# Four recurrent mixers on one Trainium2 core: three groups of small products move in the order of the engines

## What is computed

```python
p = jnp.einsum('btd,dc->btc', h, w_in[l]).astype(F32)
pa, pb, pc, pd = _split(p, MIXER_COLS)
ya = _hgrn2_mixer(pa, lb_all[l], hgrn_norm_g[l])
yb = _gla_mixer(pb, gla_gate_w2[l], gla_gate_b[l], gla_norm_g[l])
...
yc, v_first = _rwkv7_mixer(pc, v_first, v_mix, rwkv_mu[l], rwkv_w0[l], rwkv_w2[l],
...
yd = _retnet_mixer(pd, positions, log_gamma)
mix = jnp.einsum('btc,cd->btd', jnp.concatenate([ya, yb, yc, yd], axis=-1), w_out[l])
```

```python
log_f = jax.nn.log_sigmoid(g_lr @ gate_w2 + gate_b) / GLA_GATE_NORM
...
scores = jnp.einsum('bhik,bhjk,bhijk->bhij', qi, ki, decay)
out = (jnp.einsum('bhij,bhjv->bhiv', scores, vi)
       + jnp.einsum('bhik,bhkv->bhiv', qi * jnp.exp(cum), state))
```

## Time and profile before

| what | value |
|---|---|
| median of 3 runs | 3372.28 us (3362.64 to 3374.18) |
| the profiled execution | 3374.25 us, its span 3372.5 us |
| PE busy | 3001.1 us, 89% of the span |
| PEld busy | 2630.4 us, 78% |
| DVE, ACT, POOL busy | 1614.0, 1079.4 and 96.5 us |
| granted clock of PE, mean | 0.909 |
| mixer stage of layer 0 | 213.4 to 436.7 us |
| mixer stage of layer 1 | 1122.0 to 1348.2 us |
| granted clock in each of the two | 0.77 |

### The profile page before, as it was taken

How to read it: one execution, slowest core, us unless ns; L and a number is a source line. 1 busy time by engine, 2 the same in 40 slices (tenths; PEclk the granted TensorE clock), 3 DMA queues, 4 the chain that set the end, 5 groups by cost and what they waited for, 6 DMA issues and landing times. The chain is left out here.

```text
span 3372.5 us, 42029 instructions
## 1 busy us (share of the span) xinstructions
PE 3001.1 (89%) x16604; PEld 2630.4 (78%) x16604; DVE 1614.0 (48%) x2073; ACT 1079.4 (32%) x1405; POOL 96.5 (3%) x92
## 2 busy tenths in 40 slices
PE   7999977999799998769999999959999685769997
PEld 6889876878578897769999999948878574758786
DVE  3436544242443356446676767763232336542333
ACT  3334113222222331135455545542222313232222
POOL 0012100000000211000000000000000000000000
PEclk9988788999899877869999999979999896789998
DMA  4210015142232000146666666634241210141521
GB/s 147 82 40 1 1 63 138 56 131 60 66 102 76 15 1 1 63 133 184 193 191 176 190 189 193 193 100 122 70 119 38 88 35 2 55 136 44 144 59 63
DMA packets 438967, 316.87 MB, mean 94 GB/s; under 512 B 22577, under 2 KB 395313, under 8 KB 438705
## 3 DMA queue, kind: packets, MB, share of 16 engines
q1 hardware_dynamic: 438832, 314.96, 32.7%
HBM read 312.29 MB, written 2.62 MB: 93 GB/s over the span
## 5 line engine op out<-in xcount | busy, mean ns | idle before, releaser
L1424 PE MATMUL psum<-x_split,gate_up_split 128*128 128x512 f32 x1056 | 415.9, 394 | 39.2 <-DVE gate_up_split L1500 31.2
L1425 PE MATMUL psum<-x_split,gate_up_split 128*128 128x512 f32 x1056 | 414.7, 393 | 0.0
L1426 PE MATMUL psum<-x_split,gate_up_split 128*128 128x512 f32 x1056 | 414.3, 392 | 0.0
L2405 PE MATMUL psum<-x_slots_split,gate_up_split 128*128 128x320 f32 x1424 | 377.7, 343 | 7.5 <-DVE gate_up_split L2549 5.6
L1709 PE MATMUL psum<-w_split,x_split 128*128 128x256 f32 (+1 forms) x2400 | 300.7, 288 | 32.6 <-DVE w_split L1743 25.9
L1709 PEld LDWEIGHTS psum<-w_split,x_split 128*128 128x128 f32 x2400 | 296.4, 197 | 37.9 <-ACT w_split L1723 26.7
L1709 PE MATMUL psum<-x_split,w_split 128*128 128x512 f32 x1248 | 297.4, 398 | 25.1 <-DVE w_split L1743 19.9
L2406 PE MATMUL psum<-x_slots_split,gate_up_split 128*128 128x160 f32 x1424 | 314.9, 241 | 0.0
L1709 PEld LDWEIGHTS psum<-x_split,w_split 128*128 128x128 f32 x1248 | 237.2, 192 | 85.8 <-ACT w_split L1723 22.2
L1522 DVE TENSOR_TENSOR arena<-arena,psum 128x512 f32<-128x512 f32 x66 | 45.4, 688 | 530.0 <-ACT arena L1483 530.0
L2405 PEld LDWEIGHTS psum<-x_slots_split,gate_up_split 128*128 128x128 f32 x1424 | 261.9, 189 | 13.6 <-ACT gate_up_split L2490 5.8
(11 more groups left out here) (411 smaller groups left out, 4622.0 us busy)
## 6 DMA issues: line engine op xcount, KB each, us to landing
arena<-in_moe_w_gate SPq DMA_DIRECT2D x91, 512.0 KB, 4.5
arena<-in_moe_w_up SPq DMA_DIRECT2D x91, 512.0 KB, 5.8
arena<-in_moe_w_down SPq DMA_DIRECT2D x176, 256.0 KB, 3.9
arena<-in_ffn_w_gu SPq DMA_DIRECT2D x88, 512.0 KB, 5.3
arena<-in_w_in SPq DMA_DIRECT2D x36, 1024.0 KB, 5.3
arena<-in_ffn_w_down SPq DMA_DIRECT2D x132, 256.0 KB, 3.7
arena<-in_ffn_w_gate SPq DMA_DIRECT2D x22, 512.0 KB, 4.1
arena<-in_ffn_w_up SPq DMA_DIRECT2D x22, 512.0 KB, 5.5
```

The lines of the kernel that those rows point to most:

```text
L1424: nc.tensor.matmul(out, w[0], XR[:, 0, k, :], start=k == 0, stop=False)
L1425: nc.tensor.matmul(out, w[0], XR[:, 1, k, :], start=False, stop=False)
L1426: mm = nc.tensor.matmul(out, w[1], XR[:, 0, k, :], start=False, stop=k == DT - 1)
L2405: hi = lambda start, stop: nc.tensor.matmul(out, wt[0], XE[:, k8, :, :].rearrange("p s n -> p (s n)"), start=start, stop=stop)
```

## The change

Three groups of small PE work move, with what reads them, and one moves to another place in PSUM.

- `E.pe_swap` stands first on PE, ahead of `R.pe_scores(0)`.
- `L.pe_gate` and `L.dve_bias` stand behind `E.pe_state(2)` and `E.dve_state(2)`.
- `pe_diagonal` of H stands behind level 6 and ahead of `R.pe_solve_x(6)`; that of L stands ahead of level 6. Both now also wait for `corners` 1, that is for `act_take(5)`, since the diagonal now lands in bank 3, which level 5 used; before it landed in bank 1 behind the transposed keys. `act_diagonal` stands ahead of `act_take(6)`, and the two counts of `turned` and `kt_ready` change places.

```diff
--- before.py
+++ after.py
@@ -376,7 +376,7 @@
 
     def pool_diagonal(self):
         pool = self.nc.gpsimd
-        pool.wait_ge(*self.kt_ready.at(2))
+        pool.wait_ge(*self.kt_ready.at(1))
         pool.wait_ge(*self.before.o_ready.at(TT))
         heads = lambda x: x.rearrange("p (h e) -> p h e", e=HD)
         for t in range(TT):
@@ -469,16 +469,17 @@
         nc, PS = self.nc, self.k.PS
         sel = self.k.HSUM[:, 0:P:HD] if self.kd == HD else self.k.GMASK[:, 0:GROUP:HD]
         nc.tensor.wait_ge(*self.prod_ready.at(1))
+        nc.tensor.wait_ge(*self.corners.at(1))
         for c in range(TT):
             for j in range(self.T):
-                o = G_PS + 768 + c * NHEAD + j * self.hpt
+                o = G_PS + 3 * HALF + c * NHEAD + j * self.hpt
                 mm = nc.tensor.matmul(PS[:, o:o + self.hpt], self.prod[:, j * SEQ + c * P:j * SEQ + (c + 1) * P], sel, start=True, stop=True)
         mm.then_inc(*self.turned.up())
 
     def act_diagonal(self):
         nc = self.nc
-        nc.scalar.wait_ge(*self.turned.at(2))
-        nc.scalar.activation(self.dg, self.k.PS[:, G_PS + 768:G_PS + 768 + TT * NHEAD], ACT.Copy).then_inc(*self.kt_ready.up())
+        nc.scalar.wait_ge(*self.turned.at(1))
+        nc.scalar.activation(self.dg, self.k.PS[:, G_PS + 3 * HALF:G_PS + 3 * HALF + TT * NHEAD], ACT.Copy).then_inc(*self.kt_ready.up())
 
 
 class Hgrn(Decay):
@@ -591,7 +592,7 @@
         pool.wait_ge(*self.f_ready.at(1))
 
     def products_free(self, pool):
-        pool.wait_ge(*self.before.kt_ready.at(1))
+        pool.wait_ge(*self.before.kt_ready.at(2))
 
     def act_decays(self):
         nc = self.nc
@@ -1870,8 +1871,8 @@
 
             @block.tensor
             def _(pe):
+                E.pe_swap()
                 R.pe_scores(0)
-                E.pe_swap()
                 R.pe_turn(0)
                 R.pe_scores(1)
                 R.pe_turn(1)
@@ -1885,12 +1886,12 @@
                 E.pe_out(0)
                 E.pe_state(0)
                 R.pe_solve_u(1)
-                L.pe_gate(E)
                 E.pe_out(1)
                 E.pe_state(1)
                 R.pe_turn_u(1)
                 E.pe_out(2)
                 E.pe_state(2)
+                L.pe_gate(E)
                 R.pe_solve_x(2)
                 E.pe_out(3)
                 R.pe_solve_u(2)
@@ -1912,9 +1913,9 @@
                 R.pe_solve_u(5)
                 R.pe_turn_u(5)
                 H.pe_level(6)
+                H.pe_diagonal()
                 R.pe_solve_x(6)
                 H.pe_turn()
-                H.pe_diagonal()
                 R.pe_solve_u(6)
                 H.pe_out(0)
                 H.pe_state(0)
@@ -1944,10 +1945,10 @@
                 R.pe_scan_sa(3)
                 L.pe_level(5)
                 R.pe_scan_out(3)
+                L.pe_diagonal()
                 L.pe_level(6)
                 R.pe_gate()
                 L.pe_turn()
-                L.pe_diagonal()
                 L.pe_out(0)
                 L.pe_state(0)
                 for c in range(1, TT):
@@ -1987,10 +1988,10 @@
                 R.act_solve_x(5)
                 H.act_take(5)
                 R.act_turn_u(5)
+                H.act_diagonal()
                 H.act_take(6)
                 R.act_solve_x(6)
                 H.act_turned()
-                H.act_diagonal()
                 L.act_decays()
                 R.act_bare_values()
                 H.act_square()
@@ -2001,9 +2002,9 @@
                 R.act_scan_out(2)
                 R.act_scan_out(3)
                 L.act_take(5)
+                L.act_diagonal()
                 L.act_take(6)
                 L.act_turned()
-                L.act_diagonal()
                 R.act_square()
                 R.act_root()
                 L.act_square()
@@ -2021,10 +2022,10 @@
                 E.dve_state(0)
                 R.dve_solve_u(1)
                 H.dve_forget()
-                L.dve_bias(E)
                 E.dve_state(1)
                 H.dve_start()
                 E.dve_state(2)
+                L.dve_bias(E)
                 R.dve_solve_u(2)
                 H.dve_update(0)
                 E.dve_centre()
```

## The result

The changed kernel takes 3325.43 us, the median of 4 runs (3319.93 to 3329.71), against 3373.23 for four runs of the kernel before (3362.64 to 3379.14). The ratio is 0.9861, 95% interval 0.9832 to 0.9890: 48 us faster, where 3 were forecast. The profiled execution took 3326.00 us (span 3324.2), and the mean granted clock went from 0.909 to 0.929. Measured again beside the second group of the experiments, the changed kernel took 3322.52 us where the kernel before took 3363.68, which is 41 us less. Two of the ten executions of one experiment, long_wait, were in a slow state (5076 and 5077 us at a mean granted clock of 0.547) and do not count in its ratio, while its median of 3351.85 is that of all ten (3351.68 without them).

A forecast was written before the change was run, and what follows sets the result against it. The prediction took PE's order and its clock in the mixer stage as the bound. Its terms, -3.2 - 3.0 - 4.0 + 8.7, gave -1.5 us a layer, -3 for both, so 3371 us, with an 8-in-10 range of 3348 to 3383.

The forecast's parts named there:

- What bounds the kernel: Mixer stage: PE is busy nearly always, so its order and clock set the end; low-clock stretches are the main gain.
- Term 1: E.swap ahead of R.scores(0): swap and scores run faster, -3.2 us a layer, bounds -4.3 and -1.5.
- Term 2: GLA's gate moved later: the clock's fall of 6.8 us is avoided, -3 us a layer, bounds -3.4 and 0.
- Term 3: HGRN's diagonal ahead of R.solve_x(6): R.solve_u(6) at full clock, then a fall on R.scores(2)'s idle, -4 us a layer.
- rival (a): The clock holds in the HGRN part: 3355 us with one layer, 3339 with both; chance 0.31.
- Term 4: GLA's diagonal ahead of level 6: 1.7 us wait for L.act_take(5), then low clock through R.gate, +8.7 us a layer.
- rival (b): GLA's wait doesn't drop the clock, or it rises on level 6: -2 to +3 there, 3350 to 3360 us; chance 0.10.
- The sum: All four moves together: -1.5 us a layer, -3 for both, from the profiled 3374.25 us to 3371 us.
- Rival (d): The moves are hidden and the clock's falls only change places: 3374 us; chance 0.47 together with the forecast.

The follow-up runs named there:

- long_wait: Changed kernel with R.clear_later's two fills swapped and R.dve_take(2) waiting for both, lengthening PE's idle in R.scores(2): 3351.85 us, ratio 0.9959 to the kernel before.
- gate_back: Changed kernel with L.gate and L.bias alone moved back behind R.solve_u(1) and H.forget: 3321.76 us, ratio 0.9874 to the kernel before.
- hdiag_back: Changed kernel with HGRN's diagonal alone moved back behind H.turn on PE and ACT, still in bank 3: 3364.06 us, ratio 0.9995 to the kernel before.
- act_order: Changed kernel with E.act_square moved behind R.act_solve_x(3) and R.act_solved_queries ahead of H.act_root on ACT: 3337.95 us, ratio 0.9922 to the kernel before.
- ldiag_back: Changed kernel with GLA's diagonal alone moved back behind L.turn on PE and ACT: 3317.09 us, ratio 0.9866 to the kernel before.
- take5_first: Changed kernel with L.act_take(5) put ahead of R.act_scan_out(3) on ACT: 3316.45 us, ratio 0.9851 to the kernel before.
- after_again: The changed kernel itself, unedited, measured once more in the second group of experiments: 3322.52 us, ratio 0.9869 to the kernel before.
- hdiag_clear: Changed kernel with HGRN's diagonal back behind H.turn and R.clear_later ahead of L.tree on POOL: 3364.99 us, ratio 0.9995 to the kernel before.

## Why the prediction was wrong, step by step

- **What bounds the kernel**: right. The low clock of thin products on a busy PE was the time to be had, and most of the 48 us came from it (16.2 us a layer from the long stretch alone).
- **Term 1**, forecast -3.2 a layer: measured -3.5 and -3.4 at the first R.solve_x(1). The swap took 3.67 us (forecast 3.5) and the scores, from 217.48 to 221.21, 3.7 (the forecast of 3.5 took their wait as 0.1 us, where the row at 227.52 has 0.34); the reserve for a fall in a bad place wasn't needed.
- **Term 2**, forecast -3: measured -3.2 and -3.3 between R.solve_x(1) and R.solve_x(2), and gate_back loses it again at R.solve_x(2), though not in its median. R.turn_u(1), 3.62 us at half clock before, now takes 1.91:

```profile
254.87 1.91 PE L1104 MATMUL psum<-const_sb,arena 128*128 128x128 f32 x16
...
258.94 1.12 PE L569 MATMUL psum<-arena 16*128 16x512 f32 x2
```

  The rule cited there (the Trainium skill, TensorE: Matmul & The Clock Gate, Part 4: PE-mode transpose), by which the term would have been 0, is not borne out: the transposes stand where they stood, run at full clock, and the clock stays up. A plainer row stands at the start of the next stage of the kernel before, which begins with transposes alone:

```profile
436.78 6.11 PE L1598 MATMUL psum<-const_sb,arena 128*128 128x128 f32 x32 [7.26 <-PEq L1842]
```

  The clock is low when they start, behind 7.26 us of idle, and rises at 441.8 us, with nothing but transposes run since.
- **Term 3**, forecast -4: measured -16.9 and -18.6 from R.solve_u(3) to L.level(0). This is the step that failed, at the sentence "By rows 7 and 8 and the fall at 216.5 the clock most likely falls on that". All up to it was right: the fall at 325.7 had lost its cause, R.solve_u(6) ran at full clock, POOL was late by what was worked out, and the idle was 0.93 us where 1.0 to 1.2 stood. The clock held over it in both layers, which was rival (a) with its 3339. hdiag_back shows that the diagonal's place is the cause, and long_wait that with 2.65 us of idle the fall would have come as forecast. Even then the kernel took 3351.85 us and not 3371, as term 4 was off too. Why the clock held over 0.93 us here and fell over 0.92 us in act_order stays open. As for the size: (a)'s -20 was 1.4 to 3.1 too much. In layer 0 some 1.6 of the 3.1 us are a fall in and behind R.solve_u(3), which the change has and the kernel before had not (4.59 us against 3.79; at R.solve_x(6) the stage is 3.3 us behind what it had won, and 1.7 of these are only the diagonal, now ahead of it).

```profile
279.10 4.59 PE L1133 MATMUL psum<-arena 128*128 128x64 f32 x32 [1.01 <-ACT arena L1125]
```

- **Term 4**, forecast +8.7: mis-sized, measured -0.2 and -0.3 from L.level(5) to the stage's end. The wait is as worked out, and the clock does fall behind it, but for 3.4 us only, in PE's timeline:

```profile
385.97 1.03 PE L476 MATMUL psum<-keep,arena 128*128 128x4 f32 x8 [1.65 <-ACT arena L458]
386.86 2.97 PE L417 MATMUL psum<-arena 128*128 128x256 f32 x8
389.62 1.06 PE L1263 MATMUL psum<-arena 128*128 128x256 f32 x2
...
391.46 0.70 PE L1263 MATMUL psum<-arena 128*128 128x256 f32 x2
```

  Level 6 takes 2.97 us, against 1.95 and 3.73 at the two clocks, and from 391.2 R.gate runs at full speed. Up to L.dve_state(0) that costs +3.5 in either layer. The tail behind it, at half clock before, mostly holds the clock now and gives 3.7 us back. Taking "the clock falls" for "and stays down" was the error. The -0.2 lies in the bounds of rival (b), -2 to +3, but in part by luck: the 3.7 us come in ldiag_back as well, where GLA's diagonal has its old place. The move itself costs the +3.5, in all four layers of the two profiles of the changed kernel; take5_first and ldiag_back, which are without the wait, are 9 and 8 us under the changed kernel's median, and 6 and 5 under that of after_again.
- **The sum** by the measured terms: -3.5 -3.3 -16.9 -0.2 is -23.9 for layer 0 and -3.4 -3.3 -18.6 -0.3 is -25.6 for layer 1, where 1.5 us are lost again between L.level(0) and L.level(5); the stages gave -23.7 and -24.0. Rival (a) came in both layers, which the range left out, and the end of the stage stayed near its old length as in (b), a pair for which the prediction had no price. The sum also took the profiled execution's 3374.25 us as its base; from the median of 3372.28 it would have been 3369.
- **Rival (d)**: wrong as a sum, right as a picture. Small falls did change places all through the stage, and they are what hides differences of 3 us, as in gate_back.

## What to carry to other kernels

Where the granted clock of a stretch is low and PE is busy in all of it, look at what ran just before the fall: here eight products of two columns and then 64-column ones were enough, without any idle. Put thin groups between dense ones, and move whatever causes a wait of about 1 us among thin products, before counting instructions; removing a wait elsewhere can lose more than it gives as long as such a wait is left, as act_order shows. When such a fall is forecast, forecast its length from the next dense work (3.4 us where level 6 followed, 47.6 where mostly products of 64 columns or 64 rows did), not from the worst case. And when the same rows fall in one layer and hold in the other, compare how long before them the clock last rose, before calling it chance; a shift at the start of a stage does not test that.

## What the hardware showed that was not expected

- More work was faster: two dense products of 0.9 us each between HGRN's diagonal and R.solve_u(6) made the kernel 30 us faster (3364.99 to 3334.74), by their density or by the 1.8 us that they delay what follows.
- The same instructions at the same distance went at 1.2 GHz in one layer and at 2.4 GHz in the other layer of one execution (hdiag_clear), with no idle in front, so a fall isn't a property of the instruction list alone; the clock's last rise lay 33.4 us before R.solve_u(6) where it held and 31.9 where it fell.
- Once down, the clock stayed down over 34 to 48 us of work with PE busy all the time, where most of that work was products of 64 columns or 64 rows. The same work ran at full clock from start to end where it began so (309.2 to 353.5 us of the changed kernel, PE busy 40.14 of 44.30).
- An idle of 0.92 us never dropped the clock in 18 layers and always in 6, and shifting the program by 1 to 3 us changed neither. Counted from the clock's last rise, which these shifts hardly moved, the six lie apart from all 18.
- The clock rose while PE ran nothing but transposes (436.78 to 441.8 us of the kernel before).
